# One TensorE product of 512 columns issued as two of 256 columns, in a 28,735-instruction fp32 kernel

## The chip, the cores and the metric

The kernel runs on one core of one Trainium2 chip. The metric is the device time of one execution in microseconds (us). TensorE (PE in the profile) is the matrix engine: a weight load (LDWEIGHTS, shown as PEld) puts a stationary tile of up to 128x128 values into the array, and a product (MATMUL, shown as PE) streams the columns of a moving tile through it into a PSUM bank. DVE is VectorE, ACT ScalarE, POOL GpSimd, and SP SyncE, which here issues the loads of the weights.

## The reference

Two transformer-like blocks run one behind the other on 512 tokens of width 1024. What matters here is that nearly all of the arithmetic is dense fp32 products of activations with weights:

```python
def first_block(x, c, ...):
    mod = silu(c) @ w_ada + b_ada                      # shifts, scales and gates
    h = rms_norm(x, norm_mix_g) * (1 + sc1) + sh1
    proj = h @ w_in + b_in                             # glu, qk, v, o, gates, merge: 8200 columns
    y_conv = silu(layer_norm(conv31(glu))) @ w_conv_pw
    y_mlstm = sigmoid(o) * norm(mlstm_chunkwise(q, k, v, gates))
    x = x + g1 * ((g_conv * y_conv + g_mlstm * y_mlstm) @ w_out)
    h = rms_norm(x, norm_ffn_g) * (1 + sc2) + sh2
    gt, up = split(h @ w_ffn_up)                       # 1024 -> 2 x 2816
    x = x + g2 * ((silu(gt) * up) @ w_ffn_down)        # 2816 -> 1024

def second_block(x, mem, ...):
    for mixer, w_in, w_out in ((mixer_a, a_w_in, a_w_out), (mixer_b, b_w_in, b_w_out)):
        h = rmsnorm(x)
        mix, q_mem = mixer(h @ w_in)                   # top-k latent attention; banded attention
        x = x + concat(mix, memory_cross_attention(q_mem, mem)) @ w_out
        x = x + conv_glu_ffn(rmsnorm(x), f_w_up, f_conv_w, f_w_down)   # 1024 -> 2 x 2816 -> 1024
    return rmsnorm(x)
```

## The kernel before

**The form of a product.** Activations lie transposed in SBUF: 128 partitions of one feature tile, 512 tokens along the free axis. A job computes one or two output tiles of 128 features for all 512 tokens. To come near fp32 accuracy with the quick fp32r type, each operand is kept as an upper and a lower part (`w_split[p][:, 0]` and `[:, 1]`; `h_hi` and `h_lo`, or `hid_hi` and `hid_lo` for the hidden layer of a feed-forward part, `conv_*`, `a_out_*`, `b_out_*`, `mem_*`, `kv_*` elsewhere). One tile of the contraction then takes three products into the same bank, the three-pass split form: upper weight times upper activation, upper weight times lower activation, lower weight times upper activation (`for wp, hp in ((0, 0), (0, 1), (1, 0))`). Each has a stationary tile of 128x128 weights and a moving tile of 128x512 activations, and fills a PSUM bank of 128x512 fp32.

**The jobs.** `split_job` (L891) writes one job out. With two output tiles and eight contraction tiles it is 48 products; the jobs that lead back from the hidden layer have one output tile and 12 or 10 contraction tiles, 36 or 30 products. `split_product` and `late_product` run pairs of jobs in a hardware loop (`eng.Fori` in `pairs`, L414), one job for each of the two weight slots p = 0 and 1; `glu` and `qk` call `split_job` for each job, unrolled. All of these appear in the profile on L901, whichever stage they belong to. The same three products are written out in other places, where small work of TensorE is put between them: L1040 and L1059 (first two jobs), L1137 (tiles between the heads of the mLSTM), L1358 (head parts of the output projections), L1445, L1471, L1485 (queries, keys and values of mixer a) and L1533 (memory queries of mixer b).

**A form with 256 columns that is there already.** The token-major values, L1111 in the first block and L1520 in mixer b, use the same split with the operands swapped: the stationary tile is 128 tokens of `h_split`, the moving tile 256 columns of `w_split`. There the order is `for hp, wp in ((0, 0), (0, 1), (1, 0))`, so that the first two products of each three have the same stationary tile.

**What sets the order.** Each slot's weights come by DMA to `wslots`; ACT writes the upper part (L1598, L1619), POOL subtracts it for the lower part (L2719), and signals `lo_ready[p]`. TensorE waits for `lo_ready[p]` and for `bank_free[p]` (the banks have been read) ahead of a job, and signals `product_done[p]` with the last product of it. ACT may overwrite a slot's split only after `product_done[p]`. TensorE's instructions are in a fixed order written out in the program.

Of the kernel before, what the change touches and what calls it, by code (L numbers as in the profile page):

```python
# [31 lines left out]
P = 128  # L32
T = 512
# [184 lines left out]
def build(nc, io):  # L218
    ctx = ExitStack()
    with ctx:  # L220
# [624 lines left out]
        def _(pe):  # L845
# [43 lines left out]

            def split_job(p, kc, width, rhs, waits, tiles=2, split=None, between=(), late=None):  # L890
# [139 lines left out]
            def first_part(c, m):  # L1030
# [8 lines left out]
                for wp, hp in ((0, 0), (0, 1), (1, 0)):  # L1039
                    last = nc.tensor.matmul(banks[2 * p + m][:], w[wp][:, c, m * P:(m + 1) * P], h_parts(c, hp),  # L1040
                                            start=(c == 0 and wp + hp == 0), stop=(c == DT - 1 and wp == 1))
# [6 lines left out]
            def second_part(c):  # L1048
# [6 lines left out]
                for m in (1, 0):  # L1055
                    if (c, m) == (0, 0):
                        pe.wait_ge(S["norm_scaled"], DT)
                    for wp, hp in ((0, 0), (0, 1), (1, 0)):
                        last = nc.tensor.matmul(banks[2 * p2 + m][:], w2[wp][:, c, m * P:(m + 1) * P], h_parts(c, hp),  # L1059
                                                start=(c == 0 and wp + hp == 0), stop=(c == DT - 1 and wp == 1))  # L1060
# [65 lines left out]
            def tile_product(k, between=None):  # L1126
# [8 lines left out]
                for c in range(DT):  # L1135
                    for wp, hp in ((0, 0), (0, 1), (1, 0)):
                        last = nc.tensor.matmul(banks[m][:], w[wp][:, c, m * P:(m + 1) * P], h_parts(c, hp),  # L1137
                                                start=(c == 0 and wp + hp == 0), stop=(c == DT - 1 and wp == 1))
# [209 lines left out]
            def heads_part(name, j, k):  # L1348
# [6 lines left out]
                for c in range(OUT_K):  # L1355
                    pe.wait_ge(S["at_low"], before + (DT if c < DT else OUT_K))
                    for wp, hp in ((0, 0), (0, 1), (1, 0)):
                        last = nc.tensor.matmul(banks[2 * p][:], w[wp][:, c, :], out_split[name][hp][:, c, :] if c < DT else mem_split[hp][:, c - DT, :],  # L1358
                                                start=(c == 0 and wp + hp == 0), stop=(c == OUT_K - 1 and wp == 1))
# [82 lines left out]
            for i in range(2 * DT * 3):  # L1442
                m, c = divmod(i // 3, DT)
                wp, hp = ((0, 0), (0, 1), (1, 0))[i % 3]
                last = nc.tensor.matmul(banks[2 * p + m][:], w[wp][:, c, m * P:(m + 1) * P], h_parts(c, hp),  # L1445
                                        start=(c == 0 and wp + hp == 0), stop=(c == DT - 1 and wp == 1))
# [17 lines left out]
            for hd in range(A_HEADS):  # L1464
# [4 lines left out]
                for c in range(2):  # L1469
                    for wp, hp in ((0, 0), (0, 1), (1, 0)):  # L1470
                        last = nc.tensor.matmul(k_bank(hd)[:], uk[wp][:, c, hd * P:(hd + 1) * P], kv_split[hp][:, c, :],  # L1471
# [1490 lines left out]
```

## Time and profile before

| | us |
|---|---|
| median of 3 runs (2217.08 to 2217.7) | 2217.3 |
| span of the profiled execution, first to last instruction | 2216.7 |
| TensorE products, 10682 | 2197.2 busy |
| TensorE weight loads, 10682 | 1734.1 busy |
| DVE | 995.1 busy |
| ACT | 887.9 busy |
| POOL | 878.6 busy |

A product is in the record from its start to its modelled end, which lies well behind the start of the next one: a row of 0.39 us follows another by 0.23 us. So busy time and the mean of a row say little of the rate; the distance from start to start does, and over a long stretch the number of records in it. A count "(x439)" of a stretch holds every record that overlaps it, thus those that began just ahead of it too. A timeline row "x2" holds two records that follow each other.

### The profile page before, as it was taken

To read this page: it belongs to the slowest core of one execution; us is meant where nothing else is said; L and a number is where in the kernel's file an instruction comes from. 1 tells how busy PE (TensorE), PEld (TensorE's weight loads), DVE (VectorE), ACT (ScalarE), POOL (GpSimd) and SP (SyncE) were. 2 spreads that over 40 slices of the span, in tenths; PEclk is the share of its full clock that TensorE was granted. 3 is DMA by queue.
4 is the path that set the end of the run, shared out by engine and by line. 5 is a ranking of instruction groups with operands and counts; after the bars stand their busy time and mean duration, and the time that the engine had idled before them with its cause. 6 is when DMAs were issued, how large, how long until landed. Compare 5 with 4: busy or idle time off the path is not lost.

```text
span 2216.7 us, 28735 instructions
## 1 busy us (share of the span) xinstructions
PE 2197.2 (99%) x10682; PEld 1734.1 (78%) x10682; DVE 995.1 (45%) x1904; ACT 887.9 (40%) x1301; POOL 878.6 (40%) x293
## 2 busy tenths in 40 slices
PE   9999999999999999999999999999999999999998
PEld 6888977788888888775777888888786678888886
DVE  4779687473311011358984333033205933330332
ACT  3345445452432123415375443233423944422332
POOL 3443422533344444453813443443434034444433
PEclk9999999999999999999999999999999999999999
DMA  9653321225232332331202432332420034323322
GB/s 365 224 170 115 96 77 58 85 92 171 66 98 78 109 98 73 108 86 38 77 1 72 114 95 83 107 95 73 153 78 24 2 91 114 95 81 108 95 70 82
DMA packets 302200, 216.89 MB, mean 98 GB/s; under 512 B 12960, under 2 KB 287520, under 8 KB 299680
## 3 DMA queue, kind: packets, MB, share of 16 engines
q1 hardware_dynamic: 293216, 195.80, 29.6%
q10 hardware_dynamic: 8896, 19.92, 2.6%
q8 instruction: 54, 0.88, 0.2%
q14 instruction: 34, 0.28, 0.0%
HBM read 213.61 MB, written 2.10 MB: 97 GB/s over the span
## 4 chain that ended last, share of the span: by engine, by line
PE 92%; DVE 2%; issue 2%; ACT 2%; DMA 1%; POOL 1%; SPq 0%; DVEq 0%; ACTq 0%; POOLq 0%
PE bank L901 72%; PE bank L1137 4%; PE bank L1111 2%; PE bank L1332 1%; PE bank L1310 1%; PE bank L1259 1%; DMA wslots<-in_w_glu 1%; PE bank L1319 1%; PE bank L1420 1%; PE bank L1159 1%; PE bank L1288 1%; PE bank L1358 1%; PE bank L1445 1%; DVE bank L2194 1%; PE bank L1170 1%
## 5 line engine op out<-in xcount | busy, mean ns | idle before, releaser
L2719 POOL TENSOR_TENSOR w_split<-wslots,w_split 128x2048 fp32r<-128x2048 f32 (+3 forms) x177 | 732.8, 4142 | 1039.5 <-ACT w_split L1598 520.7
L901 PE MATMUL bank<-h_hi,w_split 128*128 128x512 f32 x3312 | 1043.8, 394 | 0.0
L901 PEld LDWEIGHTS bank<-h_hi,w_split 128*128 128x128 f32 x3312 | 622.3, 188 | 140.6 <-issue 7.2
L901 PE MATMUL bank<-h_lo,w_split 128*128 128x512 f32 x1656 | 646.2, 390 | 0.0
L901 PEld LDWEIGHTS bank<-h_lo,w_split 128*128 128x128 f32 x1656 | 311.0, 188 | 72.7 <-issue 3.1
L1619 ACT ACTIVATE w_split<-wslots 128x2048 fp32r<-128x2048 f32 (+2 forms) x86 | 153.4, 1783 | 461.4 <-PE bank L901 461.4
L901 PE MATMUL bank<-hid_hi,w_split 128*128 128x512 f32 x1056 | 335.0, 397 | 1.0 <-DVE hid_lo L2476 1.0
L1598 ACT ACTIVATE w_split<-wslots 128x2048 fp32r<-128x2048 f32 (+3 forms) x85 | 147.7, 1737 | 335.1 <-PE bank L901 310.8
L901 PEld LDWEIGHTS bank<-hid_hi,w_split 128*128 128x128 f32 x1056 | 198.3, 188 | 49.3 <-DVE hid_lo L2476 1.9
L901 PE MATMUL bank<-hid_lo,w_split 128*128 128x512 f32 x528 | 207.5, 393 | 0.0
L2194 DVE SCALAR_TENSOR_TENSOR bank<-arena,cols,bank 128x512 f32<-128x512 f32 x240 | 161.4, 750 | 5.8 <-ACT bank L1712 5.2
L2474 DVE TENSOR_TENSOR bank<-arena,bank 128x512 f32<-128x512 f32 x66 | 46.0, 696 | 224.4 <-ACT arena L1932 224.4
L2719 POOL TENSOR_TENSOR w_split_out<-wslots,w_split_out 128x320 fp32r<-128x320 f32 (+1 forms) x28 | 49.5, 1786 | 190.9 <-ACT w_split_out L1598 190.9
L901 PEld LDWEIGHTS bank<-hid_lo,w_split 128*128 128x128 f32 x528 | 99.0, 188 | 24.5
L2609 DVE TENSOR_TENSOR bank<-bank,rstd 128x512 f32<-128x512 f32 x44 | 30.8, 700 | 165.9 <-PE bank L901 165.5
L2433 DVE TENSOR_TENSOR xT<-xT,bank 128x512 f32 (+1 forms) x24 | 16.5, 688 | 153.2 <-PE bank L901 153.2
L1137 PE MATMUL bank<-h_hi,w_split 128*128 128x512 f32 x256 | 84.3, 399 | 0.0
L2476 DVE TENSOR_TENSOR hid_lo<-bank,hid_hi 128x512 f32 x66 | 45.7, 692 | 57.2 <-ACT hid_hi L1934 57.2
L2009 ACT ACTIVATE arena<-arena,small 128x257 f32<-128x257 f32 (+5 forms) x128 | 64.2, 503 | 17.4 <-DVE small L2551 10.5
L1934 ACT ACTIVATE hid_hi<-bank 128x512 f32 (+1 forms) x66 | 39.6, 600 | 55.6 <-DVE bank L2474 55.6
L560 DVE TENSOR_TENSOR bank<-bank,xT 128x512 f32<-128x512 f32 x24 | 16.8, 700 | 95.9 <-PE bank L901 81.3
L2614 DVE SCALAR_TENSOR_TENSOR arena<-bank,cols,arena 128x511 f32<-128x511 f32 x44 | 33.0, 750 | 58.9 <-ACT arena L1928 58.9
(369 smaller groups left out, 2713.4 us busy)
## 6 DMA issues: line engine op xcount, KB each, us to landing
wslots<-in_f_w_up SPq DMA_DIRECT2D x88, 512.0 KB, 4.8
wslots<-in_w_in SPq DMA_DIRECT2D x24, 1024.0 KB, 5.4
wslots<-in_w_ffn_up SPq DMA_DIRECT2D x44, 512.0 KB, 4.5
arena<-in_w_ada ACTq DMA_DIRECT2D x8, 2048.0 KB, 8.9
wslots<-in_f_w_down SPq DMA_DIRECT2D x16, 768.0 KB, 4.8
wslots<-in_a_w_in SPq DMA_DIRECT2D x10, 1024.0 KB, 5.4
wslots<-in_f_w_down SPq DMA_DIRECT2D x16, 640.0 KB, 4.4
arena<-in_w_ada_first SPq DMA_DIRECT2D x8, 1024.0 KB, 20.5
```

The costliest lines, as they stand in the source:

```text
L901: last = nc.tensor.matmul(banks[2 * p + m][:], w[wp][:, c, m * P:(m + 1) * P], rhs(c, hp), start=(c == 0 and wp + hp == 0), stop=(c == kc ...
L1111: last = nc.tensor.matmul(banks[2 * p + b // 2][:, (b % 2) * 2 * P:(b % 2 + 1) * 2 * P], h_split[hp][:, c, b * P:(b + 1) * P], w[wp][:, c, :],
L1137: last = nc.tensor.matmul(banks[m][:], w[wp][:, c, m * P:(m + 1) * P], h_parts(c, hp), start=(c == 0 and wp + hp == 0), stop=(c == DT - 1 ...
L1598: nc.scalar.activation(split_of(JOB_STAGE[n], p)[:, 0, 0:size], slot(p, 1, size)[:, 0, :], ACT.Copy).then_inc(hi_ready[p], 1)
L1619: nc.scalar.activation(split_of(name, p)[:, 0, 0:size], slot(p, 1, size)[:, 0, :], ACT.Copy).then_inc(hi_ready[p], 1)
L1934: nc.scalar.activation(hid[0][:, 0:tiles, :][:, 2 * i + u, :], banks[2 * p][:], ACT.Copy).then_inc(S["hid_hi_ready"], 1)
L2009: last = nc.scalar.activation(part, part, ACT.Exp, bias=stat(n, 2 * with_sink + e), scale=-1.0, accum_out=stat(n, 4 + e))
L2194: ins = nc.vector.scalar_tensor_tensor(out=acc, in0=a_pad[:, c, k:k + T], scalar=dw_w[:, c, k:k + 1], in1=acc, op0=ALU.mult, op1=ALU.add)
L2474: nc.vector.tensor_tensor(banks[2 * p][:], up_gate[:, p, :], banks[2 * p + 1][:], ALU.mult).then_inc(S["hid_made"], 1)
L2476: nc.vector.tensor_tensor(hid[1][:, 0:tiles, :][:, t, :], banks[2 * p][:], hid[0][:, 0:tiles, :][:, t, :].bitcast(F32), ALU.subtract).then ...
L2614: steps.did(nc.vector.scalar_tensor_tensor(out=acc[:, 1:], in0=gates[:, 0:T - 1], scalar=w3[:, t, 1:2], in1=acc[:, 1:], op0=ALU.mult, op1= ...
L2719: last = nc.gpsimd.tensor_tensor(part[:, 1, cols_of], slot(p, 1, size)[:, 0, cols_of], part[:, 0, cols_of].bitcast(F32), ALU.subtract)
```

## The change

Each of the nine places named above, where a product of 512 columns of the three-pass split form is issued, calls a helper instead that issues two products of 256 columns: the same stationary tile, the first and the second half of the moving tile, into the first and the second half of the bank. The flag `start` goes with the first half of the first product alone, `stop` with the second half of the last one, and a signal with the second half. The order of the work is otherwise kept, as are the waits, the other engines' programs, and the two places on L1111 and L1520.

```diff
+            def by_halves(bank, w, x, start, stop):
+
+                for lo, hi in ((0, T // 2), (T // 2, T)):
+                    last = nc.tensor.matmul(bank[:, lo:hi], w, x[:, lo:hi], start=start and lo == 0, stop=stop and hi == T)
+                return last
+
             def split_job(p, kc, width, rhs, waits, tiles=2, split=None, between=(), late=None):
...
                     for wp, hp in ((0, 0), (0, 1), (1, 0)):
-                        last = nc.tensor.matmul(banks[2 * p + m][:], w[wp][:, c, m * P:(m + 1) * P], rhs(c, hp),
-                                                start=(c == 0 and wp + hp == 0), stop=(c == kc - 1 and wp == 1))
+                        last = by_halves(banks[2 * p + m], w[wp][:, c, m * P:(m + 1) * P], rhs(c, hp),
+                                         c == 0 and wp + hp == 0, c == kc - 1 and wp == 1)
```

The other eight places change in the same way: `first_part`, `second_part`, `tile_product`, the head parts (L1358), the queries with `latent(i)` between them (L1445), keys (L1471) and values (L1485) of mixer a, and `mem_queries` (L1533).

## Rows read from the trace of the kernel before

**Rows 1.** The page's first lines: engines; TensorE's granted clock in 40 slices.
```profile
span 2216.7 us, 28735 instructions
PE 2197.2 (99%) x10682; PEld 1734.1 (78%) x10682; DVE 995.1 (45%) x1904; ACT 887.9 (40%) x1301; POOL 878.6 (40%) x293
...
PEclk9999999999999999999999999999999999999999
```

**Rows 2.** The chain that ended last, shares of the span by engine.
```profile
PE 92%; DVE 2%; issue 2%; ACT 2%; DMA 1%; POOL 1%; SPq 0%; DVEq 0%; ACTq 0%; POOLq 0%
```

**Rows 3.** L901 by operands: count, busy us, mean ns, idle before.
```profile
L901 PE MATMUL bank<-h_hi,w_split 128*128 128x512 f32 x3312 | 1043.8, 394 | 0.0
...
L901 PE MATMUL bank<-h_lo,w_split 128*128 128x512 f32 x1656 | 646.2, 390 | 0.0
...
L901 PE MATMUL bank<-hid_hi,w_split 128*128 128x512 f32 x1056 | 335.0, 397 | 1.0 <-DVE hid_lo L2476 1.0
...
L901 PE MATMUL bank<-hid_lo,w_split 128*128 128x512 f32 x528 | 207.5, 393 | 0.0
```

**Rows 4.** Whole span, one line each: L901, L1137, L1358; stretch, busy (records).
```profile
0.00:2216.70 2216.70, 1650.46 (x7104) 1332.14 (x7104) 1.00 0.32 98
...
0.00:2216.70 2216.70, 92.97 (x384) 70.78 (x384) 1.00 0.32 98
...
0.00:2216.70 2216.70, 30.49 (x120) 21.74 (x120) 1.00 0.32 98
```

**Rows 5.** Two stretches of L901 without a gap: `h_*` moving, then `hid_*` moving.
```profile
575.00:675.00 100.00, 100.00 (x439) 82.05 (x438) 1.00 0.31 87
885.00:925.00 40.00, 40.00 (x173) 32.16 (x172) 1.00 0.35 101
```

**Rows 6.** Chain in order of time: start us, us, work; two equal pairs of jobs.
```profile
55.63 22.40 PE bank L901 x96
...
78.81 22.10 PE bank L901 x96
```

**Rows 7.** Timeline, L1111, the form with 256 columns: start us, us.
```profile
228.07 0.39 PE L1111 MATMUL bank<-w_split,h_hi 128*128 128x256 f32 x2
...
229.43 0.39 PE L1111 MATMUL bank<-w_split,h_hi 128*128 128x256 f32 x2
```

**Rows 8.** Timeline, L1520, the same form in mixer b.
```profile
1685.05 0.28 PE L1520 MATMUL bank<-w_split,h_lo 128*128 128x256 f32 x1
...
1686.11 0.28 PE L1520 MATMUL bank<-w_split,h_lo 128*128 128x256 f32 x1
```

**Rows 9.** Chain in order of time: L1111 twice, L1520 twice.
```profile
234.46 21.89 PE bank L1111 x192
...
1675.95 1.38 PE bank L1520 x12
...
1678.19 1.42 PE bank L1520 x12
```

**Rows 10.** L1111 by operation: durations ns min/median/max, first and last start us.
```profile
L1111 PEld LDWEIGHTS bank<-w_split,h_hi x256: 186/188/192, 222.1 to 267.3; 128*128 128x128 f32 x128
L1111 PE MATMUL bank<-w_split,h_hi x256: 276/276/384, 222.1 to 267.4; 128*128 128x256 f32 x128
```

**Rows 11.** Timeline of the weight loads, L1332: loads of products with 128 columns.
```profile
1128.09 0.97 PEld L1332 LDWEIGHTS bank<-arena 128*128 128x128 f32 x8
```

**Rows 12.** Timeline of ACT and POOL: the split of the next weights, first feed-forward part.
```profile
643.60 1.92 ACT L1619 ACTIVATE w_split<-wslots 128x2048 fp32r<-128x2048 f32 x1 [5.84 <-PE bank L901]
...
654.59 1.92 ACT L1619 ACTIVATE w_split<-wslots 128x2048 fp32r<-128x2048 f32 x1 [5.70 <-PE bank L901]
...
645.60 4.69 POOL L2719 TENSOR_TENSOR w_split<-wslots,w_split 128x2048 fp32r<-128x2048 f32 x1 [6.29 <-ACT w_split L1619]
```

**Rows 13.** The page's DMA queues and issues: instructions; a load of weights.
```profile
q8 instruction: 54, 0.88, 0.2%
...
wslots<-in_f_w_down SPq DMA_DIRECT2D x16, 640.0 KB, 4.4
```

More of the change, by code:

```diff
@@ L1039, in first_part @@
                 for wp, hp in ((0, 0), (0, 1), (1, 0)):
-                    last = nc.tensor.matmul(banks[2 * p + m][:], w[wp][:, c, m * P:(m + 1) * P], h_parts(c, hp),
-                                            start=(c == 0 and wp + hp == 0), stop=(c == DT - 1 and wp == 1))
+                    last = by_halves(banks[2 * p + m], w[wp][:, c, m * P:(m + 1) * P], h_parts(c, hp),
+                                     c == 0 and wp + hp == 0, c == DT - 1 and wp == 1)
                 if (c, m) == (DT - 1, 1):
@@ L1357, in heads_part @@
                     for wp, hp in ((0, 0), (0, 1), (1, 0)):
-                        last = nc.tensor.matmul(banks[2 * p][:], w[wp][:, c, :], out_split[name][hp][:, c, :] if c < DT else mem_split[hp][:, c - DT, :],
-                                                start=(c == 0 and wp + hp == 0), stop=(c == OUT_K - 1 and wp == 1))
+                        last = by_halves(banks[2 * p], w[wp][:, c, :], out_split[name][hp][:, c, :] if c < DT else mem_split[hp][:, c - DT, :],
+                                         c == 0 and wp + hp == 0, c == OUT_K - 1 and wp == 1)
                     if c == OUT_K - 1:
@@ L1444, in _ @@
                 wp, hp = ((0, 0), (0, 1), (1, 0))[i % 3]
-                last = nc.tensor.matmul(banks[2 * p + m][:], w[wp][:, c, m * P:(m + 1) * P], h_parts(c, hp),
-                                        start=(c == 0 and wp + hp == 0), stop=(c == DT - 1 and wp == 1))
+                last = by_halves(banks[2 * p + m], w[wp][:, c, m * P:(m + 1) * P], h_parts(c, hp),
+                                 c == 0 and wp + hp == 0, c == DT - 1 and wp == 1)
                 if i == 2 * DT * 3 - 1:
@@ L1484, in _ @@
                     for hp, wp in ((0, 0), (0, 1), (1, 0)):
-                        last = nc.tensor.matmul(banks[6 + n % 2][:], kv_split[hp][:, c, b * P:(b + 1) * P],
-                                                uv[wp][:, c, half * T:(half + 1) * T], start=(c == 0 and wp + hp == 0), stop=(c == 1 and hp == 1))
+                        last = by_halves(banks[6 + n % 2], kv_split[hp][:, c, b * P:(b + 1) * P],
+                                         uv[wp][:, c, half * T:(half + 1) * T], c == 0 and wp + hp == 0, c == 1 and hp == 1)
                 last.then_inc(S["v_made"] if n < 2 * TB - 1 else product_done[p], 1)
@@ L1532, in mem_queries @@
                 for wp, hp in ((0, 0), (0, 1), (1, 0)):
[L1533 to L1534 removed]
+                    last = by_halves(banks[2 * p + m], mem_part[wp][:, c, m * P:(m + 1) * P], h_parts(c, hp),
+                                     c == 0 and wp + hp == 0, c == DT - 1 and wp == 1)
                 if k == 2 * DT - 1:
```

14 lines of the change are left out of this document (6 added, 8 removed).

## The prediction

> **What bounds the kernel now.** I read the page's first lines, then the chain, then the rate of TensorE's products from stretches and timelines. TensorE is busy in 2197.2 of 2216.7 us at a granted clock of 2.4 GHz throughout [rows 1], and the chain that ended last runs through it for 92% [rows 2]. No other engine is above 45%. So the time is the number of products by the distance from one start to the next. The split form on L901 hardly waits: its idle time in the whole span is 1.0 us [rows 3]. The reader is to see that the durations in those rows, 390 to 397 ns, are not the price of a product. The price stands in the counts. From 575 to 675 us 439 records overlap the stretch; 1.7 of them (0.39 us long by 0.23 us apart) began ahead of it, so 437.3 began in it, and one product of 512 columns costs 100 us / 437.3 = 228.7 ns. With `hid_*` moving it is 40 us / 171.3 = 233.5 ns [rows 5]. 512 columns at 2.4 GHz alone are 213.3 ns, so each product carries 15 to 20 ns on top, and nothing in the page says what they are. They are not fixed by place: two pairs of jobs of the same stage, with the same tiles, took 22.40 and 22.10 us for 96 products [rows 6]. There are thus at least two rhythms, a faster and a slower one, and the difference is 3 to 5 ns for each product.
>
> **How many products.** L901 has 7104 products, L1137 384, L1358 120 [rows 4]; by the code the six other places have 48 each. That makes 7896. Of them 4968 on L901 have `h_*` moving [rows 3], with L1137 and four of the small places (L1040, L1059, L1445, L1533) 5544. 1584 have `hid_*` moving [rows 3]. The other 768 are the rest of L901 (552), L1358 (120), L1471 and L1485 (96).
>
> **What the change adds.** 7896 products and as many weight loads, to the 10682 of each [rows 1]. Nothing is moved to another engine, and no wait is added; the columns streamed are the same. What is in question is one number: what two products of 256 columns cost in the place of one of 512.
>
> The trace has that form, on L1111 and L1520, with the same type and the same three passes. On L1111, from 228.07 to 229.43 us, twelve products take 1.36 us, 113.3 ns each [rows 7]; a pair would cost 226.7 ns. The rhythm holds: 192 products, with a change of bank among them, took 21.89 us, 114.0 ns each [rows 9]. On L1520 some groups run as quickly (12 products in 1.38 us), others slower (1.42 us) [rows 9], and within a slow one nine products take 1.06 us, 117.8 ns [rows 8]: a pair at 235.6 ns. So the pair's price lies between 226.7 and 235.6 ns, against 228.7 and 233.5 ns now. The bounds enclose today's price on both sides, and this is why the sign is uncertain.
>
> Whether the second load is really issued though its tile is the one that is in the array: on L1111 two products of each three have the same `h_hi` tile, and 256 loads stand beside 256 products [rows 10]. So loads are not skipped, and 113.3 ns is a price with a load for each product. A load record is 188 ns long, but this doesn't bind. The distance between loads does: eight loads of products with only 128 columns lie within 0.97 us [rows 11], of which the last takes 0.19 us, so seven distances are 0.78 us, 111 ns each. The load's own rhythm is therefore 2 ns below what the 256-column product needs. It is just hidden now, and with 512 columns half of it would have to grow before anyone noticed; after the change there is no cover left, and anything that lengthens a load lengthens the product.
>
> **Which value I take.** For the 5544 products with `h_*` moving: the faster rhythm, because these run in long stretches without a gap (439 records in 100 us [rows 5]), as L1111 does, and L1111 stayed in its faster rhythm, while the slow groups of L1520 are 12 products long and each begins behind a break. 5544 x (226.7 - 228.7) = -11.1 us. For the 1584 with `hid_*`, which are in the slower rhythm now for whole stages, I don't know which one the halves will take: faster gives 1584 x (226.7 - 233.5) = -10.8 us, slower 1584 x (235.6 - 233.5) = +3.3 us; the middle is -3.7 us. The 768 others I take at the same price per product as `hid_*`, for want of a long stretch of their own: -5.2 to +1.6, middle -1.8 us. The sum is -11.1 - 3.7 - 1.8 = -16.6 us. On the profiled execution that is 2216.7 - 16.6 = 2200.1 us; its own span lies 0.6 us below the median of 2217.3, so 2200.7 us. With both open groups fast it is -27.1 us, 2190.2; with both slow -6.2 us, 2211.1.
>
> **What the gain would meet.** ACT begins to split the next weights when a job ends, at 643.60 and at 654.59, that is 10.99 us apart, and POOL has finished at 645.60 + 4.69 = 650.29 us [rows 12]. This leaves about 4 us ahead of the moment at which TensorE has run out of the other slot's job. Jobs shorter by 1% (0.1 us) don't reach this, and a longer job hides more. The weights' loads land in 4.4 us [rows 13]. I cost all of that at nothing.
>
> The number of instructions that TensorE's sequencer must deliver doubles for a given time. It does this on L1111 already: a load and a product every 113.3 ns [rows 7]. A queue of the same number of instructions covers half the time, though, where the sequencer stops for a wait or for the turn of a loop; the trace has such stops only beside 512-column products, except on L1111, where 192 products lost 0.7 ns each to them. Bounds: nothing, and 7896 x 0.7 = 6 us.
>
> **A rule against the change.** A fixed cost for each product, independent of its columns, can be read from the rows if like rhythms are compared: 2 x 117.8 - 233.5 = 2.1 ns. The Trainium skill says the same (TensorE: Matmul & The Clock Gate, section "Wait — 56ns, not 53.3ns?"): about 2.5 ns for each warm product on top of its columns. By that page alone the pair would be 218.3 ns and the single product 215.8, both well under what the trace has, and 7896 x 2.5 ns would be 20 us more, 2237 us. The trace agrees with it on the fixed cost and contradicts its total by 13 ns or more.
>
> **The rivals.**
> (1) *The fixed cost is paid and the faster rhythm saves no more than now.* The faster rhythm saves 233.5 - 228.7 = 4.8 ns for a product of 512 columns, and 4.5 for one of 256, so it seems to be a saving for each product, and my forecast counts on getting it twice per pair. If only one half gets it, since the second goes on with the same weights, where rows show no such pair on the moving side, a pair costs 226.7 + 4.5 = 231.2 ns: 5544 x 2.5 = +13.9 us, and the other 2352 at 235.6 are +4.9: 2236 us. It decides once fewer than about three in four halves with `h_*` get the saving: 228.7 = 235.6 - n x 4.5 gives n = 1.5 of 2.
> (2) *The slower rhythm everywhere.* 5544 x 6.9 + 3.3 + 1.6 = +43 us, 2260.5 us. For it: groups of L1520 that begin behind a break stay in it for their 12 products [rows 8, 9], and the load has no cover. Against it: the long runs of L1111 [rows 9].
> (3) *The loop bodies become too long.* A pair of jobs in a loop is 96 products, about 200 instructions, and becomes 390; a fetch of instructions is 0.88 MB / 54 = 16 KB [rows 13]. If each turn of such a loop waited for a fetch, at most as long as the quickest load of weights, 4.4 us, then 27 turns (25 in the ffn up stages, two in `conv_pw` and `mix_out`) are up to 119 us: 2220 to 2336 us. The rows have no body of this length. The Trainium skill (Runtime: NRT & Kernel Launch, "Instruction fetch mechanics") gives TensorE room for 2048 instructions, by which nothing would happen, but also warns of branches beyond a window of two blocks of 256; no run here shows which holds.
> (4) *The load's rhythm alone sets the pair,* 2 x 111 = 222 ns: 5544 x 6.7 + 1584 x 11.5 + 768 x 11.5 = -64 us, 2153 us. L1111 speaks against it, being at 113.3 with the same loads.
> (5) *It doesn't do what it says:* the second load is dropped when the program is compiled. Then the pair would have cover again; [rows 10] speaks against it, and the time would lie between that of (4) and today's.
> (6) *The rhythms mix so that they cancel,* within 4.4 us of now.
>
> **How the numbers follow.** Forecast 0.46 (2190 to 2211); rival 1 0.20; rival 2 0.15; rival 3 0.06; rival 4 0.04; rival 5 0.01; rival 6 0.08. A measurement of this kernel can tell about 0.2%, 4.4 us, from no change. Faster: 0.46 + 0.04 + 0.01 = 0.51; the same 0.08; slower 0.20 + 0.15 + 0.06 = 0.41. The range reaches from the forecast's low end with 2 us for the reading of the rows, 2188, to rival 2, 2263. It leaves out rivals 3, 4 and 5, 0.11. The likeliest case alone would be 2190 to 2211 us.
>
> **What would show it.** Some 18,578 products and loads each. In the stretch from about 575 to 675 us, 885 records of products (200,000 / 226.7, and 2.4 that began ahead of it) say that the forecast's main term holds; 868 rival 1, 851 rival 2. A timeline of `hid_*` decides the second term in the same way. A gap of TensorE at every second `product_done` of an up stage, and no change of rhythm, would be rival 3. The rows of ACT L1619 and POOL L2719 should keep their 1.92 and 4.69 us. The forecast is wrong if the pairs of `h_*` are above 228.7 ns, whatever else comes out.

## The result and the profile after

Before 2217.19 us (2216.47 to 2217.70), after 2256.88 us (2256.79 to 2257.26), four runs each: ratio 1.018, 95% interval 1.0166 to 1.0195. The change costs 39.7 us. The forecast of 2200.7 us has the wrong sign; rival 2, the slower rhythm everywhere, stood at 2260.5. In the section on the experiments each ratio is taken against the kernel before as timed again beside that experiment (2217.17 to 2217.65 us).

The page of the changed kernel (engines, the queue that brings instructions, the chain, and the groups that answer [rows 3]):

```profile
span 2255.1 us, 44527 instructions
PE 2237.3 (99%) x18578; PEld 2118.8 (94%) x18578; DVE 995.6 (44%) x1904; ACT 887.6 (39%) x1301; POOL 876.5 (39%) x293
...
q8 instruction: 85, 1.39, 0.3%
...
PE 95%; issue 1%; ACT 1%; DVE 1%; POOL 1%; DMA 0%; DVEq 0%; SPq 0%; ACTq 0%; POOLq 0%
...
L893 PE MATMUL bank<-h_hi,w_split 128*128 128x256 f32 x7392 | 1198.6, 282 | 0.1
...
L893 PE MATMUL bank<-h_lo,w_split 128*128 128x256 f32 x3696 | 735.3, 280 | 0.0
...
L893 PE MATMUL bank<-hid_hi,w_split 128*128 128x256 f32 x2112 | 336.2, 280 | 0.9 <-DVE hid_lo L2482 0.9
...
L893 PE MATMUL bank<-hid_lo,w_split 128*128 128x256 f32 x1056 | 209.6, 279 | 0.0
```

There are 18,578 products and as many loads, 7896 more of each, as the prediction counted; the line is L893, since all the halves are issued in `by_halves`. TensorE still hardly waits. So the time is again count times distance, and the two stretches of [rows 5] give the distance from start to start (stretch, us; PE busy and records; PEld; granted clock; DMA share; GB/s):

```profile
575.00:675.00 100.00, 100.00 (x851) 100.00 (x850) 1.00 0.28 77
885.00:925.00 40.00, 40.00 (x342) 40.00 (x341) 1.00 0.28 82
```

851 is the very number that the prediction gave for rival 2: 2.4 records began ahead, 100 us / 848.6 = 117.8 ns for a half, 235.7 for a pair where one product took 228.7. On `hid_*` it is 40 us / 339.6 = 117.8 as well, 235.6 against 233.5. The clock was at 2.4 GHz in both kernels. PEld is now busy for the whole stretch, where it had 82 of 100 us.

Not everything went to the slower rhythm. In the chain in order of time (start us, us, work) two jobs of 48 halves are quicker than their neighbours of 96 and 84:

```profile
389.75 5.45 PE bank L893 x48
...
414.63 11.57 PE bank L893 x96
...
430.59 9.89 PE bank L893 x84
442.36 5.64 PE bank L893 x48
```

5.45 us / 48 = 113.5 ns, 11.57 / 96 = 120.5 with its entry. Read by distances between starts, seven of the 57 unbroken streams of 20 and more products of 256 columns run near 113.3 ns, 598 of 15,697 distances; nearly all others run at 117.8. Only three of the seven are made of halves on `h_*` alone (189 halves); two belong to L1117, which is L1111 of the kernel before, and two mix other halves with products of L1526, the L1520 of the kernel before. The first of L1117's three streams was itself at 117.8 here, though the change doesn't touch it. First the 84 products in the kernel before, then in the changed one:

```profile
223.86 9.81 PE bank L1111 x84
...
227.11 10.16 PE bank L1117 x84
```

With the entry that is 116.8 and 121.0 ns for each. The question was what decides between the two rhythms.

### The profile page after: what moved, and what is told of

It is laid out like the page before. It is cut to its first block, busy times and chain, and to the rows that moved or that the text cites. A ratio compares the mean times of both kernels' runs of the same rounds, so it can differ in the third digit from the quotient of the medians.

```text
span 2255.1 us, 44527 instructions
## 1 busy us (share of the span) xinstructions
PE 2237.3 (99%) x18578; PEld 2118.8 (94%) x18578; DVE 995.6 (44%) x1904; ACT 887.6 (39%) x1301; POOL 876.5 (39%) x293
## 4 chain that ended last, share of the span: by engine, by line
PE 95%; issue 1%; ACT 1%; DVE 1%; POOL 1%; DMA 0%; DVEq 0%; SPq 0%; ACTq 0%; POOLq 0%
PE bank L893 81%; PE bank L1117 2%; PE bank L1338 1%; PE bank L1316 1%; PE bank L1265 1%; PE bank L1325 1%; PE bank L1426 1%; PE bank L1165 1%; PE bank L1294 1%; PE bank L1176 1%; PE bank L1526 0%; POOL w_split_out L2725 0%; PE bank L974 0%; PE bank L1005 0%; DMA xT<-in_x 0%
## 5 line engine op out<-in xcount | busy, mean ns | idle before, releaser
L893 PE MATMUL bank<-h_hi,w_split 128*128 128x256 f32 x7392 | 1198.6, 282 | 0.1
L893 PEld LDWEIGHTS bank<-h_hi,w_split 128*128 128x128 f32 x7392 | 1006.7, 188 | 29.2 <-issue 28.7
L893 PE MATMUL bank<-h_lo,w_split 128*128 128x256 f32 x3696 | 735.3, 280 | 0.0
L893 PEld LDWEIGHTS bank<-h_lo,w_split 128*128 128x128 f32 x3696 | 564.8, 188 | 4.6 <-issue 4.6
L893 PE MATMUL bank<-hid_hi,w_split 128*128 128x256 f32 x2112 | 336.2, 280 | 0.9 <-DVE hid_lo L2482 0.9
L893 PEld LDWEIGHTS bank<-hid_hi,w_split 128*128 128x128 f32 x2112 | 285.8, 188 | 1.3 <-DVE hid_lo L2482 1.3
L893 PE MATMUL bank<-hid_lo,w_split 128*128 128x256 f32 x1056 | 209.6, 279 | 0.0
L893 PEld LDWEIGHTS bank<-hid_lo,w_split 128*128 128x128 f32 x1056 | 161.6, 188 | 0.0
L1316 PE MATMUL bank<-arena 64*128 64x256 f32 (+5 forms) x256 | 54.4, 417 | 0.9 <-ACT arena L2113 0.7
```

The source lines that it names most:

```text
L893: last = nc.tensor.matmul(bank[:, lo:hi], w, x[:, lo:hi], start=start and lo == 0, stop=stop and hi == T)
L1316: last = nc.tensor.matmul(score_bank(g0 + g, e)[:, 0:n], q, kk, start=True, stop=True)
```

## The experiments

The letters of the theories are those that the expectations give them. Where a series stands behind the kernel's last product, its rhythm is the mean of its last six distances between starts, read in the trace. Each kernel with such series was executed once. An "entry" is the way a series begins: behind a pause of eight products of one column, and with its first product whole or cut at some column.

**Series behind the last product.** Does the halved form reach 113.3 ns on the tiles of `h_*` at all, and does the order or the size of the parts matter?

```
+ for wp, hp in ((0, 0), (0, 1), (1, 0)):      # abridged, as are the cuts of code below
+     for lo, hi in cuts:            # 512; 256+256; half-major; 384+128; 320+192; ...
+         matmul(banks[7][:, lo:hi], w_split .. [:, c, 0:P], h_split[hp][:, c, lo:hi])
```

> The kernel before, and behind its last product series of extra products on two of its tiles into a free bank, so that the price of a form is measured by itself: 24 products each of 512 columns; the same as 256+256; as 256+256 with the three passes first for one half, then for the other; as 384+128; as 320+192; as four times 128; again 512 and 256+256, all on one pair of tiles; 24 bf16 products of 512, 256 and 128 columns. The output is the reference's; the time is longer by the extra work. Theory A (streaming runs at about 0.451 ns a column whatever the form, a fixed cost of about 2.2 ns for each product, and a distance of at least 111 ns between loads): 512 costs 233 ns, or 229 in the faster rhythm; 256+256 235.6 or 226.7; 384+128 is 175.6+111 = 287; 320+192 is 146.7+111 = 258; four times 128 is 444 to 450. Theory B (the loads' rhythm of 113 to 118 ns bounds the 256-column product, and its streaming would be quicker): 384+128 is then 175.6+118 = 294 and the 128-column products are 118 ns apart in the slower rhythm. If the 15 to 20 ns above 213.3 belong to 4-byte moving data, bf16 products of 512 columns cost about 216 ns; if they belong to every product, about 229.

Chain in order of time; the first five series are 512, 256 + 256, the same with the halves outermost, 384 + 128, 320 + 192, and the last line is that of bf16 products of 512 columns:

```profile
2209.93 5.61 PE bank L1585 x24
...
2217.22 5.77 PE bank L1585 x48
...
2224.67 5.76 PE bank L1585 x48
...
2232.11 6.93 PE bank L1585 x48
...
2240.77 6.25 PE bank L1585 x48
...
2288.99 5.12 PE bank L1599 x23
```

Per product of 512 columns: 228.8 ns whole, 117.8 + 117.8 as halves in either order, 226 + 61 = 287 for 384 + 128 and 169 + 88 = 257 for 320 + 192, as theory A added them up. In these two the load behind the small part starts 108 to 109 ns after the small part's own load, never sooner. On one pair of tiles it is 229.0 and 117.8 again. So the kernel's numbers come back without its other work, and loads of fp32r products keep a distance of about 110 ns. The bf16 series answer the other question of the expectation: 215.8 ns for 512 columns, 109.2 for 256, 55.8 for 128. Most of the 15 to 20 ns above the 213.3 of the columns thus belong to the 4-byte products. The series with four parts of 128 columns fell into the lower clock and gives no price; it is shown in the last section.

**Entries.** Sixteen series of halves, alike but for the cut of their first product.

```
+ for first in (256, 252, 248, 244, 240, 232, 224, 208, 192, 160, ...):
+     apart(); pairs_of(24, first)   # product 0 cut at `first`, the others at 256
```

> The kernel before, and behind its last product 32 series of 24 pairs of 256 columns on the same tiles. The first pair of each is cut at another column (256, 252, 248, 244, 240, 232, 224, 208, 192, 160, 128, 64, 264, 272, 288, 320); the first 16 series begin behind eight tiny products, the other 16 follow each other without a break. Output as the reference's. Theory A (the rhythm is chosen by the phase in which a stream begins, and kept): some cuts give 113.3 ns a product throughout their series and others 117.8, and in the second part, too, a cut changes the rhythm. Theory B (these tiles' addresses choose it): all 32 series run at the same distance. Theory C (two products with the same weights in a row exclude the faster rhythm): all at 117.8.

```profile
2217.91 5.55 PE bank L1593 x48
...
2225.14 5.76 PE bank L1593 x48
...
2247.47 5.57 PE bank L1593 x48
```

The first cuts 252, 232 and 192 gave 113.3 ns for the whole series, the other thirteen 117.8. In the part without breaks, the cut 128 + 384 turned a slow stream fast and the next cut, 64 + 448, turned it back; the other fourteen left it slow. The rhythm is a phase that lasts once it is there; what hangs on the pair of halves alone can't explain it. The three fast series also have pairs with the same weights throughout, so theory C falls here.

**Halves outermost in the kernel.**

```
- for wp, hp in passes: by_halves(...)
+ for lo, hi in ((0, T // 2), (T // 2, T)):
+     for wp, hp in passes: matmul(..[:, lo:hi], ..)
```

> The changed kernel, with the order in the split jobs turned: for each contraction tile the three passes over the first half of the columns, then the three over the second, so that no weight tile is loaded twice in a row but for the two passes with the upper weights. Theory C (the repeated tile, or the continuation into the second half, excludes the faster rhythm): most jobs at 113.3 ns, 2190 to 2200 us. Theory A (fixed cost and a rhythm that isn't bound to the order): 117.8 ns stays, 2250 to 2262 us.

2260.56 us, ratio 1.019 [1.0177, 1.0208]: no gain, theory A. The order was turned in `split_job` alone. Having fewer neighbours that share their stationary tile does not bring the faster rhythm; why it is 3.7 us slower than the changed kernel was not followed.

**Halves in the jobs of one output tile only** (1584 products on `hid_*`, and 384 of the output projections and gates).

```
+ cuts = ((0, T // 2), (T // 2, T)) if tiles == 1 else ((0, T),)
```

> The kernel before, with halves in the jobs of one output tile alone (the way back from the hidden layer, 1584 products, 360 of the output projections, 24 of the gates). Those of the hidden layer are in the slower rhythm before (233.5 ns). Theory A (only a fixed cost of 2.2 ns, rhythm slow in both): +3.5 us and about +1 for the others, 2221 to 2223 us. If the halves also lose something of their own where the stage changes, more than that.

2221.97 us, ratio 1.002 [1.0011, 1.0030], 4.3 us above before. The stretches are those of before and of after:

```profile
575.00:675.00 100.00, 100.00 (x439) 82.04 (x438) 1.00 0.33 91
885.00:925.00 40.00, 40.00 (x342) 40.00 (x341) 1.00 0.36 104
```

1584 x (235.6 - 233.4) = 3.5 us for `hid_*`, and the rest of the 4.3 fits the 384 other products. What is left of the loss, 35 us, lies on the other products, `h_*` above all.

**Other cuts in the kernel,** to turn its streams.

```
+ kick=(0, 1, 128)   # glu jobs 2 to 7, second job of each late pair: contraction tile 1 begins 128 + 384
+ kick=(0, 0, 252)   # qk jobs: the first product cut 252 + 260
```

> The changed kernel with another first cut in some jobs, nothing else: in the glu jobs 2 to 7 and in the second job of each late product (ahead of the loops of the ffn up stages with a late norm) the first product of the second contraction tile is cut 128+384 in place of 256+256; in the eight qk jobs the very first product is cut 252+260. Both cuts brought series of pairs into the faster rhythm in the last experiment. Theory A (the rhythm is a phase, set at a stream's entry and kept): some jobs, or all of a kind, now run at 113.3 ns a product and stay there to the end of the job, and where it happens ahead of a loop the whole loop does: each glu or qk job so gained is 96 x 4.4 ns = 0.4 us, each up loop some 4 us or more; 2230 to 2256 us. If the rhythm depends on more than that, all stays at 117.8 and 2257 us.

2254.70 us (ratio 1.017 [1.0151, 1.0185]), 2.2 below the changed kernel. 13 streams of 69 are fast, 1324 distances, among them a stream of 304 halves; the streams of 3239 and twice 2638 in the feed-forward parts stayed at 117.8. Another cut can turn a stream, but not dependably.

**Entries on other tiles.** Whole products on `h_*`, whole products on `hid_*`, halves on `hid_*`, sixteen first cuts each.

> The kernel before, and behind its last product 48 series of 18 products, each series behind eight tiny products and with a first product cut at another column (none, 252, 248, 244, 240, 232, 224, 208, 192, 160, 128, 64, 264, 272, 288, 320): 16 series of 512 columns on h tiles, 16 of 512 columns on the hidden layer's tiles, 16 of 256+256 on the hidden layer's. Output as the reference's. Theory A asks why the h stages of 512 columns were nearly always in the faster rhythm and those of 256 nearly never: if it is the number of phases that lead into it, then most of the 16 series of 512 on h reach 228.9 ns and none or few on hid (233.3), and few of the 256+256 on hid reach 113.3. If instead the kernel's surroundings decide, the 512 series on h split as the 256 ones did, about one in five fast.

Whole on `h_*`: 228.9 ns from all sixteen. Whole on `hid_*`: 233.3 from fifteen, 231.2 from one. Halves on `hid_*`: 117.8 from all. So in these series whole products fall into nearly one rhythm whatever the entry, and which one depends on the tiles. That was the thing to follow.

**Operands crossed.**

> The kernel before with forty short series of split products behind its last product, each of 18 products behind a pause of eight one-column products: ten configurations with four entries each (first product whole, or cut at column 252, 192 or 128; in the halved ones at 256, 252, 192, 128). (1) 512 columns, stationary tiles of w_down, moving tiles of h_split, passes high-high, high-low, low-high; (2) 512, w_in with hid_split, same order; (3) 512, w_down with hid_split, passes high-high, low-high, high-low; (4) 512, w_in with h_split in that order; (5) halves, w_in with h_split in that order; (6) halves, w_in with h_split, every second product begun with its right half; (7) 512, w_in with hid_split in the other order; (8) halves, w_in with hid_split; (9) steady cuts 252 + 260; (10) 240 + 272. The series write a bank nobody reads. If the moving tile decides which rhythm a 512-column product ends in (theory M): (1) and (4) 228.9 ns, (2), (3), (7) 233.3. If the stationary tile decides (S): (2) and (7) 228.9, (1) and (3) 233.3. If the pass order decides (O), (3) and (4) differ from the last run's 233.3 and 228.9. For halves: if the rhythm is a phase set at entry that nothing corrects, 117.8 each for most entries in (5), (6), (8), 113.3 for a few; if an uneven steady cut corrects it, (9) or (10) gives 226.7 a pair for all four entries, else 235.6 for most. The kernel takes some 2217 + 40 x 18 x 0.23 = 2383 us plus the pauses, so about 2420.

With `h_*` moving 228.8 to 229.0 in eight of eight, whichever weights and order of passes; with `hid_*` moving 233.3 in ten of twelve and 231.2 in two. Theory M holds, S and O fall. Of the twelve series of halves three were fast, all on `h_*`, from entries that differ with the order of the products: 252 in (5), 192 and 128 in (6), none in (8). The steady cuts 252 + 260 gave 116.7 a half (233.3 a pair) from every entry, 240 + 272 gave 117.5 to 119.

**The place of the moving tile.** The tiles are moved by bytes.

```
+ def moved(tile, floats):
+     flat = tile[:].rearrange("p c n -> p (c n)")[:, floats:floats + 6 * T]
```

> The kernel before with 52 short series behind its last product, each of 18 products behind eight one-column products, stationary tiles of w_split throughout, passes high-high, high-low, low-high; thirteen configurations of moving tiles with four entries each (first product whole, or cut at 252, 192 or 128). By the allocation the four moving tiles start at bytes 32896 (h_hi), 112512 (h_lo), 128896 (hid_hi) and 194624 (hid_lo) of a partition; the first three are multiples of 128, hid_lo is 64 beyond one. Configurations: (1) h_hi with h_lo, (2) hid_hi with h_lo, (3) h_hi with hid_lo, (4) h_hi with h_lo moved by 64 bytes, (5) h_hi moved by 64 with h_lo, (6) hid_hi with hid_lo moved by 64, (7) both h tiles moved by 64, (8) both moved by 32, (9) h_hi moved by 128, (10) h_hi alone in all passes, (11) hid_lo alone, (12) halves on hid_hi with hid_lo moved by 64, (13) steady cuts 224 + 288 on h. If the start address of the low tile decides the rhythm (theory A128): 228.9 ns a product in (1), (2), (6), (9), (10) and 233.3 in (3), (4), probably (5), (7), (8) and (11). If it is the pair of tiles by something else than their place to 128 bytes (theory N): (6) stays at 233.3 and (4) at 228.9. (12): halves at 117.8 for most entries in either theory, and a fast one by a few; (13) 226.7 a pair in all four if a cut at a multiple of 128 bytes beyond the middle corrects the phase, else 235.6 for most. The whole kernel: 2217 + 52 x (18 x 0.231 + 1.9) = about 2530 us.

The entries "whole" and 252 of configuration 3 (`h_hi` with `hid_lo` as it is), then those of configuration 6 (`hid_hi` with `hid_lo` 64 bytes further):

```profile
2257.48 4.30 PE bank L1601 x18
...
2263.47 4.30 PE bank L1601 x19
...
2329.23 4.24 PE bank L1601 x18
...
2335.15 4.23 PE bank L1601 x19
```

In the rhythm that is 233.3 (one of four entries 231.2) against 228.8 to 229.0: 64 bytes on one tile do it, and `hid_hi` is as good as `h_hi`. But (9), `h_hi` moved by 128, was 229.5 to 232.3, so 128 isn't the modulus; and (11) had 226.7 from all four entries, quicker than any 512-column product in the kernel. Of the others, (1), (2) and (10) had 228.8 to 229.0, (4) and (5), with one of the two tiles moved, 228.8 to 232.3, (7) 232.5 to 233.3, (8), with both tiles moved by 32 bytes, 233.3; (12) had one fast series of halves in four; and the steady cuts of (13) were slower, 123 to 124 ns a part. `hid_lo` lies 64 beyond a multiple of 256, as `w_split` does. Theory A128 was too narrow.

**The grid.** Moving tiles by 0, 64, 128, 192 bytes and stationary ones by 0, 64, 128, 192, whole and halved.

> The kernel before with 64 short series behind its last product, 18 split products each behind eight one-column products, h_split as moving tiles and w_split as stationary ones, high-high, high-low, low-high. First 32 series of 512 columns, then 32 of 256 + 256; in each half the stationary tiles are read from 0, 64, 128 and 192 bytes beyond their start and, within that, both moving tiles from 0, 64, 128 and 192 bytes beyond theirs, with two entries each (first product whole, or cut at 192). Where they start, counted from a multiple of 256 bytes: w_split 64, h_hi and h_lo 128, hid_hi 128, hid_lo 64. The last run had 228.9 ns a product with both moving tiles at 128, 226.7 with one moving tile at 64 in all passes, 229.7 to 232.3 with both at 192, and 233.3 where one was at 64 and one at 128. If the rhythm goes by the distance between moving and stationary tile (theory R): 226.7 wherever moved bytes of h = moved bytes of w + 192 (mod 256), and each value of that difference has one rhythm in all four rows. If it goes by the moving tiles' own place (theory P): 226.7 in every case with h moved by 192, whatever w. If neither (theory L, the tiles' whole addresses or their number), no such order in the grid. Halves: if the place sets them too, the same cells have 113.3 ns from both entries; if the entry alone sets them, 117.8 in most cells, without order. The whole kernel: 2217 + 64 x (18 x 0.231 + 1.9) = about 2605 us.

Sorted by distance, that is the moving tile's start less the stationary tile's, modulo 256 (eight series in each cell):

| distance, bytes | whole, ns | half, ns |
|---|---|---|
| 0 | 226.7 | 120.0 |
| 64 | 228.8 to 229.0 | 117.8, one 113.3 |
| 128 | 232.3 to 233.2 | 118.0 to 120.0 |
| 192 | 233.3 | six 113.3, two 117.8 |

Halves with `w_split` unmoved: both entries at distance 64, one at 192, one at 0 (36 products each):

```profile
2401.60 4.36 PE bank L1602 x36
...
2407.63 4.37 PE bank L1602 x36
...
2425.82 4.20 PE bank L1602 x36
...
2437.62 4.42 PE bank L1602 x36
```

All 32 whole series are where theory R puts them, and P and L fall: the four rows of the grid are the same row shifted. For halves the distance says which rhythms there are, and at 64 and 192 the entry chooses.

In the grid both moving tiles have the same distance. The kernel before has `hid_hi` at 64 and `hid_lo` at 0, and its 233.3 ns is more than either of the two has alone (228.9 and 226.7). So a mixture isn't the mean of its parts, and the table holds only where all parts share one distance.

**`hid_lo` 64 bytes further, in the kernel before.**

```
- taken[0] = PROBS_AT
+ taken[0] = PROBS_AT + 16
  hid.append(split_region("hid_lo", HALVES[0][1], T))
```

> The kernel before (512-column products everywhere), with the tile hid_lo placed 64 bytes further, so that hid_hi, hid_lo, h_hi and h_lo all start 128 bytes beyond a multiple of 256. Nothing else differs. If the place of the low tile decides the rhythm (as the series of the last run say), the 1584 products on hid fall from 233.3 to 228.9 ns: 1584 x 4.4 = 7.0 us less, 2210 us, ratio 0.9968. If the series behind the kernel's end don't stand for the loops (other engines reading and writing beside them), 2217, ratio 1.000.

2210.87 us, ratio 0.997 [0.9958, 0.9981], 6.7 us below before for 7.0 expected. The stretch with `hid_*` has 176 records where [rows 5] had 173:

```profile
885.00:925.00 40.00, 40.00 (x176) 32.81 (x176) 1.00 0.39 118
```

This kernel also answers the open point of [rows 6]. Its `h_*` tiles lie as before, yet the first of those two equal pairs of jobs is quick here:

```profile
55.02 21.98 PE bank L901 x96
```

It was 22.40 us in the kernel before, where 149 whole products on `h_*` in a row, these among them, ran 233.3 ns apart. So the entry chooses for whole products too, at distance 64: of the traces with `h_*` and `w_split` unmoved and whole products on them, only that of the kernel before has this slow stream, while a short stream of 24 products on L1137 is at 233 ns in every one.

**Distance 0 in the kernel before.**

```
+ taken[0] += 16
  w_split_at = taken[0]
```

> The kernel before (512-column products) with 64 bytes of space ahead of w_split, so that w_split and all that lies behind it, hid_lo among it, starts 64 bytes further: w_split, h_hi, h_lo, hid_hi and hid_lo then all start 128 bytes beyond a multiple of 256, distance 0 between moving and stationary tile. Nothing else differs. If the distance decides the rhythm in the loops as in the series (theory R): h 228.9 -> 226.7 ns on 4968 + 384 products, -11.8 us; hid 233.3 -> 226.7 on 1584, -10.6; the 480 products of L1111 and L1520, which have w_split as moving tile, 113.3 -> 120.0, +3.2 us: 2217 - 19 = 2198 us, ratio 0.991. If the place of h and hid alone decides (theory P): as the kernel with hid_lo moved, 2211.

2198.11 us, ratio 0.991 [0.9896, 0.9929], on the number expected. All 36 streams of 20 and more whole products on `h_*` end at 226.7 here, the one on L1137 too. 443 and 177 records: 100 us / 441.3 = 226.6 ns and 40 / 175.3 = 228.2 on `hid_*`, where the stream has a break near the end of the stretch and the settled products are at 226.7:

```profile
575.00:675.00 100.00, 100.00 (x443) 82.81 (x442) 1.00 0.33 92
885.00:925.00 40.00, 40.00 (x177) 32.84 (x176) 1.00 0.34 102
```

**Distance 192, halves and whole.** `taken[0] += 32` ahead of `w_split_at`, and `PROBS_AT + 48` for `hid_lo`; once in the changed kernel, once in the kernel before.

> The changed kernel (halves) with 128 bytes of space ahead of w_split and 192 more ahead of hid_lo: the moving tiles h_hi, h_lo, hid_hi and hid_lo at 128 and w_split at 192 beyond a multiple of 256, a distance of 192 where it was 64 (h) or 64 and 0 (hid). In the series halves at this distance ended at 113.3 ns in 6 of 8, at 117.8 in 1 of 8 at distance 64. If the distance decides (theory R): 14256 halves on h and hid by 4.44 ns for three quarters of them, -47 us, for all of them -63; the 480 products of L1111 and L1520 go to 117.8, +2.1: 2194 to 2212 us, faster than the kernel before. If only the entry sets the halves' rhythm (theory A as it stood after the first runs): 2257 us, as the changed kernel.

> The kernel before (512-column products) with the same places as the run before this one (distance 192). Theory R: h 228.9 -> 233.3 ns on 5352 products, +23.8 us, hid stays at 233.3, L1111 and L1520 +2.1: 2243 us, ratio 1.012. Then the same change, 512 -> 256 + 256, made at these places, is a gain of 31 to 49 us instead of a loss of 40. Theory P or no effect: 2217.

Whole: 2240.61 us, ratio 1.011 [1.0088, 1.0122], 2243 expected. Halves: 2248.35 us (2243.33 to 2252.72), ratio 1.013 [1.0115, 1.0149]: neither the 2194 to 2212 of theory R nor the 2257 of A. First the two stretches of the whole form, then those of the halves:

```profile
575.00:675.00 100.00, 100.00 (x430) 80.59 (x429) 1.00 0.31 84
885.00:925.00 40.00, 40.00 (x173) 32.23 (x172) 1.00 0.28 82
```

```profile
575.00:675.00 100.00, 100.00 (x852) 100.00 (x851) 1.00 0.31 84
885.00:925.00 40.00, 40.00 (x342) 40.00 (x341) 1.00 0.30 87
```

The whole form is at 100 us / 428.3 = 233.5 ns, as the grid has it. The halves took the slow one of their two rhythms in the long streams again; 17 streams of 56, 1351 distances, took the fast one. Of the streams on `h_*` alone, 15 of 37 were fast, the longest of 182 halves, where the changed kernel had 3 of 38. So distance 192 does bring the fast rhythm more often, but not into the stages that hold most of the products. The four executions lie 9.4 us apart, where those of the other kernels timed in as many runs lie within 1.5, and the traced one is the slowest of them. This fits a rhythm chosen at entries, but the share of the fast one was mis-sized: six of eight in the series, about one product in twelve in the traced execution.

**Distance 0, halves.** `taken[0] += 16` in the changed kernel.

> The changed kernel (halves) with the same 64 bytes of space ahead of w_split as in the run that brought whole products to 226.7 ns: distance 0 for every product on h and hid. In the series halves at this distance ran at 120.0 ns from all eight entries. If the distance decides the halves' rhythm in the loops too (theory R): 14256 halves by +2.2 ns, +31.4 us, and the 480 products of L1117 and L1526 from mostly 113.3 to 120.0, +2 to +3: 2257 + 34 = 2291 us, ratio to the kernel before 1.033, and to whole products at the same places (2198.1 us) 1.042. If only the entry decides (theory A): 2257, ratio 1.018.

2292.66 us, ratio 1.034 [1.0323, 1.0357], for 2291 expected:

```profile
885.00:925.00 40.00, 40.00 (x335) 40.00 (x335) 1.00 0.22 66
```

40 us / 332.6 = 120.3 ns. Against whole products at the same places it is 2292.66 - 2198.11 = 94.6 us, and 7128 x (240.0 - 226.7) = 94.8, from the two rhythms of the grid and the products on `h_*` and `hid_*` alone; summed in the two traces it is +68.7 on `h_*`, +20.2 on `hid_*` and some 5.5 on the 768 others, so the match to 0.2 us is partly luck.

## Why the prediction was wrong

**The step that failed** is "Which value I take". It gave the 5544 products on `h_*` the 113.3 ns of L1111, because both run in long stretches without a gap, and had -11.1 us from them. They ran at 117.8 ns a half, and the distances on `h_*` summed in the two traces went from 1294.6 to 1326.5 us, +31.9.

The length of a stretch is not what decides: in the changed kernel 3239 halves ran without a break, all at 117.8. What the row of L1111 could not give is that halves have two lasting rhythms, that the entry chooses between them, and that the placement of the tiles sets which there are and how often each comes. L1111 reads `w_split` as moving and `h_split` as stationary tile, a distance of 192 bytes; the products of L901 read them the other way, a distance of 64. The placement runs moved L1111's own operands too (L1112 there, since a line was added ahead of it). Its second stream, 192 products, took 21.89 us in the kernel before [rows 9]. Here it is in the kernel of whole products with `w_split` 128 bytes further, where this line has distance 64, and in the one with `w_split` 64 bytes further, where it has distance 0:

```profile
236.49 22.72 PE bank L1112 x192
...
231.89 23.13 PE bank L1112 x192
```

Over all traces of this case the three streams of that line were at 113.3 ns in 33 of 36 at distance 192, at 117.8 in six of six at 64, and at 120.0 in six of six at 0. The row was of the same type, size and passes and still of another case. L1520 has the distance of L1111 and has both rhythms [rows 8, 9], as the grid has at 192.

The distance is not the whole reason, though. With `h_*` at 192 the long streams of halves stayed at 117.8 all the same, so the forecast's value would have failed for them there too. What in an entry leads to one rhythm or the other is open.

**The size.** Rival 2's terms come to 43 us, of which `h_*` has 5544 x 6.9 = 38; 39.7 were measured. The spans of the two traced executions differ by 38.4 us, and the summed distances account for it: +31.9 on `h_*`, +3.4 on `hid_*`, +2.6 on the 768 others, +0.3 on L1111. The term on `h_*` is smaller than rival 2's since its settled whole products take 228.9 ns and not 228.7, 149 of them were in the slow rhythm already, three streams of halves were fast, and the distances with a break in them grew less.

**`hid_*`.** Its open choice, -6.8 or +2.1 ns a pair, fell to the second: 3.4 us in the traces for 3.3. The middle taken, -3.7 us, was not one of the two outcomes that it weighed.

**The rule against the change.** Its 2 x 117.8 - 233.5 = 2.1 ns was the loss on `hid_*`. But it paired the slow rhythms of two forms and called them like, and by the grid they aren't one cost: a pair of halves against a whole product is +6.7 ns at distance 64, -6.7 or +2.3 at 192 and +13.3 at 0. For fp32r products no fixed cost can thus be told apart from the rhythms. The Trainium skill's figure (TensorE: Matmul & The Clock Gate, "Wait — 56ns, not 53.3ns?"), about 2.5 ns a product, gave 2237 us; the bf16 series agree with it (2 x 109.2 - 215.8 = 2.6 ns), and the kernel has twice that loss. The prediction's words that the trace contradicts the skill's total by 13 ns or more hold for the whole product (228.7 against 215.8); for the pair of L1111 it is 226.7 against 218.3, 8.4 ns.

**The rivals.** (1) 868 records were expected, 851 seen; the streams on `h_*` are settled at 117.8 or at 113.3, and none holds a pair of one and the other. (3) refuted: 3239 halves in loops without a gap, though the queue of instructions shows 85 packets instead of 54 [rows 13]. (4) refuted: the quickest streams of halves have 113.3 ns. (5) refuted by 18,578 loads. (6) didn't happen.

**What was costed at nothing** was nothing. The next weights' splits, by operation (count, durations ns, first and last start), keep the durations of [rows 12], 11.3 us apart for 10.99:

```profile
L1625 ACT ACTIVATE w_split<-wslots x2: 1914/1914/1914, 642.8 to 654.1; 128x2048 fp32r<-128x2048 f32 x2
```

```profile
L2725 POOL TENSOR_TENSOR w_split<-wslots,w_split x2: 4675/4675/4675, 644.8 to 656.1; 128x2048 fp32r<-128x2048 f32 x2
```

**What the sign rests on.** With whole products 2217, 2241 and 2198 us and halves 2257, 2248 and 2293 at the three placements tried, halving costs 39.7, 7.7 and 94.6 us. So the size of the loss belongs to the placement, and a gain was found at none. The best rhythm of a pair, 2 x 113.3, is no better than the best of a whole product, 226.7, which whole products took in every series and every stream on `h_*` at distance 0. The kernel with distance 0 is 19 us quicker than the one before, by one line.

**Open:** by what path the places of the two tiles act on each other, and why with a period of 256 bytes; why long streams at distance 192 take the slow rhythm so much more often than the series did; what rhythm tiles with different distances fall into; whether steps finer than 64 bytes would do better (the one tried, 32 bytes, gave 233.3 ns).

## What to carry to other kernels

When TensorE never waits and its products still cost more than their columns, look at the start addresses: for fp32r products of 512 columns, put every moving and every stationary tile at the same offset modulo 256 bytes, the low parts too, and measure the rhythm as records in a long stretch. Do not carry a rhythm from one line of a profile to another that reads other tiles, even with the same type, size and order. Splitting products gained at none of the three placements tried, and at two of four distances it leaves the rhythm to the entry; do it only where a whole product can't be used.

## What the runs showed of the hardware

**Placement of tiles.** The same 512-column product takes 226.7 to 233.3 ns by the distance of its two tiles modulo 256 bytes, and a 256-column one 113.3 to 120.0, in the opposite order at 0 and 192. It shows with the other engines idle: in the grid's kernel DVE, ACT and POOL had no instruction from 2215 to 2590 us. The Trainium skill (SBUF — State Buffer, "Who interferes with whom") says that PE waits on no other engine, and lists two independent read ports for it, one for the moving operand and one for weights; no run here tests the first. As to the second, the grid shows that the place of one operand against the other changes the time of a product; whether the ports have a part in it no run shows.

**Phases that last.** Halves held 117.8 ns over 3239 products and 113.3 over 304. Whole products at distance 64 held 228.9 in most streams and 233.3 over 149 products in one; at distance 0 all were at 226.7 by their last distances.

**The clock.** In the first series kernel the granted clock fell to half, 1.2 GHz, 1.0 us after the series with four parts of 128 columns had begun, at 2249.6 us. TensorE had been busy without a gap before it, with the 320 + 192 series and eight products of one column. The distance went from 111.9 to 213.3 ns:

```profile
2252.00:2262.00 10.00, 10.00 (x49) 10.00 (x48) 0.00 (x0) 0.00 (x0) 0.00 (x0) 0.50 0.00 0
```

It stayed at 1.2 GHz for 27.3 us, into the next series of 512 columns, whose products were 426.6 ns apart until it rose. This was seen once, and what made it fall is not shown. The long stretches of halves shown above all have a granted clock of 1.00.
